# Lower parts of one upward tile per group of the small expert items made by GpSimd instead of VectorE

## The reference

```
def moe_ffn(h, router_w, router_b, w_gate, w_up, w_down):    # 8 experts, top 2, hidden width 3584
    ...
    top_vals, top_idx = lax.top_k(logits, TOP_K)
    top_w = jax.nn.softmax(top_vals, axis=-1)
    gates = jnp.sum(jax.nn.one_hot(top_idx, N_EXPERTS, dtype=jnp.float32) * top_w[..., None], axis=1)
    for e in range(N_EXPERTS):
        y = swiglu_2(t, w_gate[e], w_up[e], w_down[e])       # (silu(t @ w_gate) * (t @ w_up)) @ w_down
        out = out + gates[:, e:e + 1] * y
```

## Time and profile before

| | us |
|---|---|
| median of 3 runs (lowest, highest) | 2671.87 (2670.59, 2681.54) |
| the profiled execution | 2670.39 |
| its span, first to last instruction | 2668.6 |
| VectorE busy in the span | 2020.8 |
| TensorE busy in the span | 2522.3 |
| mean granted TensorE clock | 0.985 of full |

### The profile page before, as it was taken

One profiled execution on the slowest core, in us unless ns is written; L12 is line 12 of the kernel. 1 busy time (PEld: TensorE's weight loads), 2 busy tenths in 40 slices (PEclk: granted clock), 3 DMA queues, 4 the chain that ended last, 5 costly groups with the idle time before them and its releaser, 6 DMA issues.

```text
span 2668.6 us, 45484 instructions
## 1 busy us (share of the span) xinstructions
PE 2522.3 (95%) x17582; PEld 2135.5 (80%) x17601; DVE 2020.8 (76%) x1962; ACT 1497.9 (56%) x1519; POOL 89.3 (3%) x82
## 2 busy tenths in 40 slices
PE   8999999999999999999999999998899899888987
PEld 7888898888889898888889987776787678666855
DVE  6666877666666866667666756989888998998898
ACT  5443524445443515445446734678767776786676
POOL 6000006000000000000000000000000000000000
PEclk9999999999999999999999999999999999999998
DMA  8665313555564314564565413999999999999993
GB/s 280 191 183 178 117 35 127 189 189 175 190 208 144 101 35 158 189 200 159 189 189 156 149 47 120 381 349 362 366 349 343 366 366 347 351 371 334 326 367 142
DMA packets 342893, 601.45 MB, mean 225 GB/s; under 512 B 11984, under 2 KB 180816, under 8 KB 342608
## 3 DMA queue, kind: packets, MB, share of 16 engines
q1 hardware_dynamic: 335264, 590.85, 64.6%
q10 hardware_dynamic: 7472, 8.35, 0.9%
HBM read 598.11 MB, written 1.05 MB: 225 GB/s over the span
## 4 chain that ended last, share of the span: by engine, by line
DMA 34%; PE 34%; DVE 18%; DVEq 7%; ACT 4%; issue 2%; another core or an unknown queue 0%; ACTq 0%; SPq 0%; PEld 0%; PEldq 0%
DMA raw<-in_ffn_w_down 12%; DVE wlo L316 12%; PE ps L567 6%; DMA raw<-in_w_in 6%; DVEq L318 6%; DMA raw<-in_moe_w_up 5%; DMA work<-in_moe_w_gate 4%; PE ps L591 4%; PE ps L570 3%; ACT whi L312 3%; PE ps L2983 3%; PE ps L856 2%; PE ps L3027 2%; PE ps L2988 1%; DMA raw<-in_moe_w_gate 1%
## 5 line engine op out<-in xcount | busy, mean ns | idle before, releaser
L316 DVE TENSOR_TENSOR wlo<-raw,whi 128x2048 fp32r<-128x2048 f32 (+1 forms) x394 | 901.9, 2289 | 183.3 <-ACT whi L312 172.3
L312 ACT CAST whi<-raw 128x2048 fp32r<-128x2048 f32 (+1 forms) x394 | 751.4, 1909 | 380.9 <-DMA raw<-in_ffn_w_down 142.6
L567 PE MATMUL ps<-xboth,whi 128*128 128x512 f32 x1680 | 420.8, 392 | 0.0
L2983 PE MATMUL ps<-whi,xboth 128*128 128x512 f32 x1344 | 352.7, 398 | 5.1 <-issue 3.9
L567 PEld LDWEIGHTS ps<-xboth,whi 128*128 128x128 f32 x1680 | 305.3, 189 | 57.1
L2983 PEld LDWEIGHTS ps<-whi,xboth 128*128 128x128 f32 x1344 | 246.3, 188 | 59.0 <-issue 7.8
L316 DVE TENSOR_TENSOR wlo<-U,whi 128x2048 fp32r<-128x2048 f32 x112 | 256.2, 2287 | 25.2 <-ACT whi L312 18.3
L2988 PE MATMUL ps<-wlo,xboth 128*128 128x512 f32 x896 | 248.0, 399 | 15.1 <-DVE wlo L316 12.8
L312 ACT CAST whi<-U 128x2048 fp32r<-128x2048 f32 x112 | 213.7, 1912 | 54.1 <-DMA U<-in_moe_w_up 44.1
L570 PEld LDWEIGHTS ps<-xboth,wlo 128*128 128x128 f32 x1680 | 229.2, 190 | 16.4
L570 PE MATMUL ps<-xboth,wlo 128*128 128x256 f32 x1680 | 234.2, 282 | 0.0
(11 more groups left out here) (586 smaller groups left out, 3738.9 us busy)
## 6 DMA issues: line engine op xcount, KB each, us to landing
raw<-in_moe_w_gate SPq DMA_DIRECT2D x58, 1024.0 KB, 6.2
raw<-in_moe_w_up SPq DMA_DIRECT2D x56, 1024.0 KB, 6.8
U<-in_moe_w_up SPq DMA_DIRECT2D x56, 1024.0 KB, 6.8
U<-in_moe_w_down SPq DMA_DIRECT2D x56, 1024.0 KB, 6.4
raw<-in_ffn_w_gate SPq DMA_DIRECT2D x55, 1024.0 KB, 5.4
raw<-in_ffn_w_up SPq DMA_DIRECT2D x55, 1024.0 KB, 5.4
raw<-in_ffn_w_down SPq DMA_DIRECT2D x55, 1024.0 KB, 5.0
work<-in_moe_w_gate SPq DMA_DIRECT2D x54, 1024.0 KB, 6.5
```

The costliest lines, as they stand in the source:

```text
L312: act.copy(whi[:, n % SPLIT, 0:width], buf[:, 0:width]).then_inc(hi_ready[n % RAW], 1)
L316: dve.tensor_tensor(wlo[:, n % SPLIT, 0:width], buf[:, 0:width], whi[:, n % SPLIT, 0:width], ALU.subtract).then_inc(split_ready[n % SPLIT], 1)
L567: pe.matmul(ps[:, first_bank + b, :], whi[:, n % SPLIT, c * GW + b * P:c * GW + (b + 1) * P], xboth[:, c].rearrange("p a t -> p (a t)"), s ...
L2983: pe.matmul(dst, part[:, rows, xhalf(q)], whi[:, (m + k) % SPLIT, c * EW:(c + 1) * EW], start=(rows == 0 and part is xhi), stop=False)
```

## The change

In the small items, the lower part of tile 3 of a group (the second up tile) is made by GpSimd. `is_aside` names these tiles: six in each small item, those that the small item's own loop over groups works on. VectorE leaves them out. ScalarE's copy of such a tile raises another semaphore, for GpSimd alone. TensorE, which elsewhere starts on the upper part once that is there, waits for the lower part of an aside tile before it starts on either. A new function `moe_pool` runs on GpSimd: a loop with the same count, and in it six subtractions, each with its drain that frees the buffer. Two semaphores whose stage is past are used again (`aside_hi`, and `pairs_known`, by which VectorE tells GpSimd that the count of pairs is in SBUF).

```diff
-        def split_hi(act, n, width=TILE, landed=16, slot_of=raw_slot):
+        def split_hi(act, n, width=TILE, landed=16, slot_of=raw_slot, ready=None):
...
-            act.copy(whi[:, n % SPLIT, 0:width], buf[:, 0:width]).then_inc(hi_ready[n % RAW], 1)
+            act.copy(whi[:, n % SPLIT, 0:width], buf[:, 0:width]).then_inc(ready or hi_ready[n % RAW], 1)
...
+        ASIDE = [ITEM_TILES + 6 * g + 3 for g in range(EN - 1)]
+
+        def is_aside(n, m):
+            return m >= n + 4 and (m - n - 4) % (2 * ITEM_TILES) in ASIDE
...
             def upper(m):
-                if m not in first_tiles:
+                if m in first_tiles or is_aside(n0, m):
+                    take_split(pe, m)
+                else:
                     pe.wait_ge(hi_ready[m % RAW], 1)
-                else:
-                    take_split(pe, m)
 
             def lower(m):
-                if m not in first_tiles:
+                if m not in first_tiles and not is_aside(n0, m):
                     take_split(pe, m)
                     pe.sem_clear(hi_ready[m % RAW])
...
+            def upper_part(m):
+                split_hi(act, m, slot_of=slot_of, ready=f["aside_hi"] if is_aside(n0, m) else None)
...
             def refill(m, end):
-                if m < end:
+                if m < end and not is_aside(n0, m):
                     dve.wait_ge(hi_ready[m % RAW], 1)
                     split_lo(dve, m, slot_of=slot_of)
...
             overflow_vector(dve)
+            dve.sem_inc(f["pairs_known"], 1)
...
+        def moe_pool(pool, n):
+
+            slot_of = moe_slots(n)
+
+            def aside_parts():
+                for g in ASIDE:
+                    m = n + 4 + g
+                    buf, _, free_ = slot_of(m)
+                    take(pool, f["aside_hi"])
+                    pool.tensor_tensor(wlo[:, m % SPLIT, :], buf, whi[:, m % SPLIT, :],
+                                       ALU.subtract).then_inc(split_ready[m % SPLIT], 1)
+                    pool.drain().then_inc(free_, 1)
+
+            pool.wait_ge(f["pairs_known"], 1)
+            pairs = pool.value_load(ids[0:1, PAIRS_AT:PAIRS_AT + 1], min_val=E // 2 - 1, max_val=SLOTS // 2 - 1)
+            with long_loop(pool, pairs):
+                aside_parts()
+            aside_parts()
...
+            moe_pool(pool, first_tile["moe"])
```

More of the change, by code:

```diff
@@ L2672, in build @@
         final_row = mt(D)
+        f["aside_hi"] = f["pool_u0"]
+        f["pairs_known"] = f["pool_u"]
         FAR_AT = WORK - 2 * TILE
@@ L2960, in moe_tensor @@
         def moe_tensor(pe, n, l):
+            n0 = n
             first_tiles = range(n, n + SPLIT)
             def upper(m):
-                if m not in first_tiles:
+                if m in first_tiles or is_aside(n0, m):
+                    take_split(pe, m)
+                else:
                     pe.wait_ge(hi_ready[m % RAW], 1)
-                else:
-                    take_split(pe, m)
             def lower(m):
-                if m not in first_tiles:
+                if m not in first_tiles and not is_aside(n0, m):
                     take_split(pe, m)
@@ L3123, in next_split @@
                 if m + SPLIT < end:
-                    split_hi(act, m + SPLIT, slot_of=slot_of)
+                    upper_part(m + SPLIT)
             def low_copy(bank, low):
@@ L3136, in gated @@
                     act.activation(sil[:, g % 2, :], ps[:, 4, :], ACT.Silu)
-                split_hi(act, m + 1 + SPLIT, slot_of=slot_of)
+                upper_part(m + 1 + SPLIT)
             def raised(m, g, end, q):
@@ L3449, in build @@
         STREAM["moe"], TENSOR["moe"], VECTOR["moe"], SCALAR["moe"] = moe_stream, moe_tensor, moe_vector, moe_scalar
+        first_tile = {}
         block = ctx.enter_context(nc.Block())
@@ L3460, in _ @@
             for part in SECOND_PLAN:
+                first_tile[part] = n
                 n = STREAM[part](sp, n, None)
```

## The result

| | this kernel | before, same chip | ratio (95% interval) |
|---|---|---|---|
| first measurement | 2716.17 us | 2676.46 us | 1.0160 (1.0146 to 1.0175) |
| again, beside the experiments | 2719.81 us | 2671.05 us | 1.0175 (1.0156 to 1.0194) |

What follows compares the result with a forecast made beforehand. VectorE was taken to bound the small items; 24 groups losing 1.99 us each add 47.8 us to the profiled 2670.39 us, giving 2718.2, and with 1.5 us up to the median, 2720 us (1.8% slower). Range 2681 to 2757 us.

Steps and rivals of the forecast that it cites:

- What bounds small items: Small items: VectorE has no time left; each lower part moved away takes 2.43 us of its queue per group.
- GpSimd's price: One 128x2048 two-input subtraction on GpSimd: taken as 4.7 us, between ends of 3.1 and 5.9 us.
- Exclusion over the whole operation: Aside tiles: GpSimd's subtraction and VectorE's two-input lower part each stand still until the other is through, for 4.7 us too.
- Rival A: Aside tiles: long operations run side by side without holding each other; 2661 us, or 2626 with cheap GpSimd; chance 0.08.
- The size of that term: Small-item groups with an aside tile: VectorE loses 4.7 - 0.28 - 2.43 = 1.99 us each, with nothing hiding it.
- rival B: Small items: TensorE, idle about 2 us a group more, drops to half clock; 48 us more, 2768 us; chance 0.06.
- TensorE's new wait: Aside tiles: TensorE's wait for GpSimd's lower part is hidden by 0.8 us, since the turned rows come later; no cost.
- 24 x 1.99: All four small items: 24 aside tiles at 1.99 us each, 47.8 us in total.
- What to see in the profile: Signs: 24 GpSimd rows of 4 to 5.5 us, held lower parts of 4.5 to 6.5, groups of 17.9, large items unchanged.

Runs made afterwards that it cites:

- e5_narrow: Changed kernel, but GpSimd makes only 16 of the 2048 columns of each aside lower part: 2631.84 us, 0.9840 of the kernel before.
- e11_late_filled: Changed kernel, GpSimd filling zeros for about 4.5 us, then making only 16 of 2048 columns, plus ten idle TensorE products: 2668.17 us, 0.9977 of before.
- e9_before_filled: Kernel before, with six idle TensorE products ahead of its wait for the turned rows in small items: 2668.80 us, 0.9978 of before.
- e2_beside: Kernel before, all lower parts on VectorE, plus a 128x1792 GpSimd multiplication per aside tile that nobody waits for: 2752.67 us, 1.0296 of before.
- e3_fill_beside: Kernel before, all lower parts on VectorE, plus a 128x1792 GpSimd zero fill per aside tile that nobody waits for: 2680.56 us, 1.0026 of before.
- e10_late: Changed kernel, but GpSimd fills zeros for about 4.5 us, then makes only 16 of 2048 columns of each aside lower part: 2683.04 us, 1.0037 of before.
- e7_filled: Changed kernel, with ten idle TensorE products where it waits for GpSimd's lower part: 2698.86 us, 1.0091 of before.
- e1_upper_at_once: Changed kernel, but TensorE starts on an aside tile's upper part at once, with an added ScalarE drain: 2718.83 us, 1.0173 of before.
- e8_large: Changed kernel with aside tiles in large instead of small items, TensorE starting on their upper parts at once: 2709.91 us, 1.0135 of before.

## Why the prediction was right, and where it was not

**What bounds small items: right, nearly.** Taking 2.43 us per group off VectorE gained 1.3 us a group in the small items (`e5_narrow`, 31 us; 29 against the kernel before with idle products), so VectorE was the bound by that much; where there is a gather, the next path is only 0.3 us behind. What comes next can be seen in the group above: VectorE, done at 2141.49, waits 1.58 us for ScalarE's upper part.

**GpSimd's price: right.** 4.55 us alone (the row at 2063.90) against 4.7 taken. The figure of the Trainium skill (GPSIMD Engine Reference, section "Performance versus the Vector engine"), 4.497 us, is the closer one; the trace agrees with it.

**Exclusion over the whole operation: right**, and the step without which the change would cost about nothing (`e11_late_filled` 0.9977 against `e9_before_filled` 0.9978). Shown by the row at 2143.07, by `e2_beside` (82 us without any dependence, 66 of them held lower parts) and by `e3_fill_beside` and `e11_late_filled`, where GpSimd fills for 1.60 and 4.27 us and VectorE's lower parts keep their 2.29 us. The rule of the Trainium skill (SBUF — State Buffer, section "SBUF: two separate sides") holds for a long operation too, with the exception for operations that read nothing, which it also states. Rival A is refuted by the held rows. Its case is `e10_late` and `e11_late_filled`, which give 1.0037 and, at the higher clock, 0.9977 (it had 0.996, 10 us less than before; the answer is 0.24 us later here, up to 6 us in 24 tiles); the kernel that really subtracts gives 1.016.

**The size of that term: too large, by a hand-over and a neighbour.** Predicted 1.99 us a group. At full clock, `e7_filled` against `e9_before_filled`, it is 1.72, 0.97, 1.70, 1.73 and 1.73 us. In four of five this is 4.55 - 2.43 - 0.41 = 1.71: the two hand-overs overlap by 0.41 us (as in `e2_beside`), not 0.28. In one group `add_back` (0.75 us, with an input in PSUM) stands between the two lower parts and runs while GpSimd holds the other one, which takes 5.58 us; I had written that nothing falls into that time. VectorE and GpSimd in that group of `e7_filled`:

```profile
2100.61 0.75 DVE L3258 SCALAR_TENSOR_TENSOR x<-ps,work,x 128x512 f32<-128x512 f32 x1 [0.24 <-remote]
2101.37 5.58 DVE L316 TENSOR_TENSOR wlo<-raw,whi 128x2048 fp32r<-128x2048 f32 x1
```

```profile
2098.56 6.24 POOL L3388 TENSOR_TENSOR wlo<-raw,whi 128x2048 fp32r<-128x2048 f32 x1 [13.61 <-ACT whi L312]
```

Five of the six aside tiles of an item lie in these distances, 7.85 us; the first, ahead of them, costs 1.7 to 1.9 us as well. In all, the small items are 38.6 us longer at full clock (448.4 against 409.8), 1.61 us a tile, where 47.8 us and 1.99 were predicted. The two kernels differ by only 30 us (2698.86 against 2668.80), because 6.4 us come back in the stretch behind the loop and 1.5 us elsewhere, of which the prediction knows nothing.

**The clock: 13 to 17 us that the sum does not have.** This is rival B, which I had priced at 48 us and given 0.06. It neither took over nor stayed away. In the changed kernel TensorE waits 2.88 us at one place, ahead of 2146.05, and the products that follow run at 1.2 GHz in some groups, as here at 2164.52 (1.71 us for four products, against 1.19 at 2146.05):

```profile
2164.52 1.71 PE L2991 MATMUL ps<-whi,xboth 128*128 128x512 f32 x4 [2.88 <-POOL wlo L3386]
2166.02 1.91 PE L2996 MATMUL ps<-wlo,xboth 128*128 128x512 f32 x4
```

The windows say the same: 0.95 in the stage, 0.89 in this small item. Filling the wait takes 18 to 22 us off, in the kernel before 6. So the total is right partly by luck. In the profiled executions the small items grew by 51.0 us (412.0 to 463.0): 38.6 us for which the term "24 x 1.99" had 47.8, so that it is 9 us too large, and 12.4 us of clock, for which the sum had nothing. Outside of them some 6 us came back. The three errors leave 44.6 us between the two spans (2668.6 and 2713.2), beside the 48 us forecast.

**TensorE's new wait: covered, as said.** The 0.8 us of cover is seen at full clock: at 2148.88 TensorE still waits for the turned rows, 0.72 us. Where the clock is low the cover is gone: the down products behind the turned rows of 2129.44 start at 2130.61, 0.75 us after those are ready (0.16 us in the earlier trace rows, 2111.76 and 2111.92). `e1_upper_at_once` shows that starting on the upper part at once gains next to nothing (2718.83 against 2719.81 us).

**What to see in the profile: nearly all as listed.** 24 GpSimd rows of 4.55 to 6.60 us where 4 to 5.5 were named: the time waited for VectorE stands in GpSimd's row. In this item the held lower parts have 4.3 to 6 us, and the groups 18.5 to 19.8 us where 17.9 was named. The first three small items grew by 12.3 to 12.8 us each, the fourth by 13.1 up to its sixth group, within the 10 to 14 that were named. What lies outside the small items kept its length within 3 us, but for the stretch behind the loop, 5.8 us shorter.

## What to carry to other kernels

Before a two-input elementwise operation is moved from a full VectorE to GpSimd, look in the trace for rows of the two that overlap: here VectorE gave up 2.4 us and then made no lower part for GpSimd's 4.5 us, less 0.4 for the hand-overs and less what VectorE does meanwhile with an input in PSUM. Ask too what the relief is worth by itself: a run in which GpSimd does next to nothing (`e5_narrow`) put it at 1.3 of the 2.4 us, and the late answer alone took that back. A longer wait of TensorE costs by itself and once more by the lower clock of the products behind it, so price both, or fill the wait with idle products (0.2% even in the kernel before). Slack by busy share is not slack on a chain: `e8_large` lost 35 us with an engine that had 16 of 125 us free.

## What the runs showed that I had not expected

- A gain far from the change: with the aside tiles off VectorE, three groups of the fourth large item take 55.5 to 57.8 us instead of 63.6 to 66.5. Its cause is open.
- A GpSimd fill of 128x1792 fp32 (1.60 us) leaves VectorE's two-input operations at 2288 ns; a multiplication of the same size, 3.17 us alone, adds 2.76 us to three of them. The fill reads nothing and the multiplication does; a GpSimd operation with one input was not tried.
- GpSimd's two-input operation with both inputs the same region took 3.17 us for 1792 columns, 1.77 ns a column; with two different inputs 4.55 us for 2048, 2.22 ns a column. That the shared input is the reason was not tested.
- Idle products that keep TensorE from waiting raise the granted clock of the expert stage from 0.95 to 0.99 (`e7_filled`) and from 0.97 to 0.99 (`e9_before_filled`).
